# Keys and values of the memory formed before its norm's root, and the steps around them reordered

## The reference

```python
h = rmsnorm(x, g_mix);  mem_n = rmsnorm(mem, g_mem)
proj = h @ w_in                       # HGRN2 | dilated attention | memory queries | three gates
kv = mem_n @ w_mem_kv                 # keys and values of the memory, 4 heads of 128 each
p_m = softmax(q_m @ k_m^T * 128**-0.5);  o_mem = p_m @ v_m
f = lb + (1 - lb) * sigmoid(z)        # lb: softmax over two rows of logits, per direction
x = x + merged @ w_out                # merged: three branches, each with its sigmoid gate
x = x + PEER(rmsnorm(x));  out = rmsnorm(x)
# rmsnorm(x, g) = x * rsqrt(mean(x * x) + 1e-6) * g, the mean over the 2048 features
```

## Time and profile before

| | |
|---|---|
| median of three runs | 4317.9 us |
| profiled execution | 4321.06 us, span 4319.3 us, mean granted TensorE clock 0.992 |
| TensorE (PE) busy | 4240.2 us, 98% |
| its weight loads (PEld) | 3881.8 us, 90% |
| DVE | 2501.7 us, 58% |
| ACT | 1574.3 us, 36% |
| POOL | 2529.4 us, 59% |
| DMA | 870.50 MB, 202 GB/s on average |

### The profile page before, as it was taken

One profiled execution on the slowest core, in us unless ns is written; L12 is line 12 of the kernel. 1 busy time (PEld: TensorE's weight loads), 2 busy tenths in 40 slices (PEclk: granted clock), 3 DMA queues, 4 the chain that ended last, 5 costly groups with the idle time before them and its releaser, 6 DMA issues.

```text
span 4319.3 us, 67486 instructions
## 1 busy us (share of the span) xinstructions
PE 4240.2 (98%) x24940; PEld 3881.8 (90%) x24940; DVE 2501.7 (58%) x3662; ACT 1574.3 (36%) x2079; POOL 2529.4 (59%) x1276
## 2 busy tenths in 40 slices
PE   7999999999999999999999999999989999999998
PEld 7878788888887877888899999999989999999998
DVE  5422443455535433897477777777762467766655
ACT  5222333333334433222344444444433332333332
POOL 5333344444443444444588888887008898898773
PEclk9999999999999999999999999999999999999999
DMA  7695566666667874233355555555365799999983
GB/s 251 203 382 170 152 202 186 192 187 189 190 189 225 269 228 136 88 97 120 118 123 136 132 123 135 131 134 133 122 214 175 274 342 336 333 345 349 346 297 108
DMA packets 574119, 870.50 MB, mean 202 GB/s; under 512 B 85648, under 2 KB 423952, under 8 KB 556944
## 3 DMA queue, kind: packets, MB, share of 16 engines
q1 hardware_dynamic: 401536, 591.47, 42.9%
q0 software_dynamic: 77824, 134.52, 11.7%
q10 hardware_dynamic: 94608, 142.52, 9.3%
HBM read 784.55 MB, written 218.04 MB: 232 GB/s over the span
## 4 chain that ended last, share of the span: by engine, by line
PE 80%; issue 9%; POOL 6%; DVE 2%; DMA 2%; ACT 1%; ACTq 0%; POOLq 0%; DVEq 0%; SPq 0%
PE banks L2076 18%; PE banks L2077 18%; PE banks L2078 18%; PE banks L2413 7%; PE banks L2414 7%; PE banks L2412 7%; POOL w_lo L682 4%; POOL w_lo L738 1%; PE banks L2277 1%; DMA arena<-expert_rows_scratch,constants 1%; POOL constants L720 0%; DVE arena L1391 0%; DMA constants<-gelu_scratch 0%; PE banks L2372 0%; DMA w_raw<-w_u 0%
## 5 line engine op out<-in xcount | busy, mean ns | idle before, releaser
L2076 PE MATMUL banks<-x_hi,w_hi 128*128 128x512 f32 (+1 forms) x4800 | 1777.0, 370 | 29.9 <-DVE x_lo L1997 13.2
L2077 PE MATMUL banks<-x_lo,w_hi 128*128 128x512 f32 (+2 forms) x4928 | 1798.3, 365 | 0.0
L2078 PE MATMUL banks<-x_hi,w_lo 128*128 128x512 f32 (+1 forms) x4800 | 1761.4, 367 | 0.0
L682 POOL TENSOR_TENSOR w_lo<-w_raw,w_hi 128x1024 fp32r<-128x1024 f32 x364 | 898.7, 2471 | 1436.3 <-ACT w_hi L752 1232.3
L752 ACT ACTIVATE w_hi<-w_raw 128x1024 fp32r<-128x1024 f32 x612 | 644.8, 1058 | 1070.2 <-PE banks L2078 1000.1
L2076 PEld LDWEIGHTS banks<-x_hi,w_hi 128*128 128x128 f32 x4800 | 904.8, 188 | 144.6 <-DVE x_lo L1997 14.9
L2077 PEld LDWEIGHTS banks<-x_lo,w_hi 128*128 128x128 f32 x4928 | 931.4, 189 | 104.5 <-issue 1.2
L2078 PEld LDWEIGHTS banks<-x_hi,w_lo 128*128 128x128 f32 x4800 | 904.7, 188 | 109.7
L705 POOL DMA_INDIRECT gate_matrix_scratch<-arena,constants x384 | 741.5, 1931 | 116.9 <-issue 116.9
L738 POOL TENSOR_TENSOR w_lo<-w_raw,w_hi 128x1024 fp32r<-128x1024 f32 x252 | 611.0, 2433 | 133.6 <-ACT w_hi L752 131.3
L2414 PE MATMUL banks<-x_hi,w_lo 128*128 128x256 f32 x1664 | 470.8, 283 | 0.0
(11 more groups left out here) (291 smaller groups left out, 4527.1 us busy)
## 6 DMA issues: line engine op xcount, KB each, us to landing
expert_rows_scratch<-w_v SPq DMA_DIRECT2D x256, 512.0 KB, 5.2
w_raw<-w_u SPq DMA_DIRECT2D x256, 512.0 KB, 3.7
w_raw<-w_v SPq DMA_DIRECT2D x256, 512.0 KB, 5.1
w_raw<-w_in SPq DMA_DIRECT2D x200, 512.0 KB, 3.7
gelu_scratch<-arena ACTq DMA_DIRECT2D x126, 256.0 KB, 2.5
gate_matrix_scratch<-early_mix_or_one_hots SPq DMA_DIRECT2D x16, 1536.0 KB, 9.7
constants<-gelu_scratch ACTq DMA_DIRECT2D x128, 192.0 KB, 6.3
early_mix_or_one_hots<-gate_matrix_scratch ACTq DMA_DIRECT2D x32, 768.0 KB, 10.7
```

The lines of the kernel that those rows point to most:

```text
L682: nc.gpsimd.tensor_tensor(wlo[s][:], raw[s][:], whi[s][:], ALU.subtract).then_inc(w_lo_made, 1)
L2076: M.matmul(out, whi[s][:, k], h, start=f, stop=False)
L2077: M.matmul(out, whi[s][:, k], l, start=False, stop=False)
L2078: ins = M.matmul(out, wlo[s][:, k], h, start=False, stop=e)
```

## The change

The gain of the memory's norm is still multiplied into each tile before it is rounded, in ACT's rounding itself; the root is left out of the tiles. It is one number per memory token, so it is multiplied into the keys and values as they are copied out of PSUM, now by DVE (`key_value_out`), from a copy of the spread root in SBUF (`mem_root`). The squares of the memory are taken two tiles at a time, 512 columns, after the first weights have been rounded; its mean is taken by TensorE behind half 4 of the `w_kv` stream and spread behind half 5 (chunk `c == 2`), the input's mean behind half 8 and spread behind half 9 (`c == 4`). The first key chunks are formed one at a time, in banks 0, 1, 6, 5, 0, 1, 0, 1. The memory's operands move: low parts into the early mix buffers, high parts into the last eight tiles of `xlo`, so the input's first eight low parts need no wait for `w_kv`. All of the memory's low parts are made by DVE. The copies of chunks 4 to 7 stand between DVE's operations on the input. Parameters and first constants are queued between the two halves of the memory. The lower bounds' first six operations move behind the input's norm, their exponential before the memory attention, the last seven behind it.

The core of the diff (left out: imports of names, semaphore lists and the memory attention's neighbours, which do not change):

```diff
+KV_BANK = [0, 1, 6, 5, 0, 1, 0, 1]
+        mlo = nc.alloc_sbuf_tensor_at("memory_low", [P, KT, MEM], F32R, offset=nc.sbuf_base - 4 * HT * T)
-        mhi = xlo[:, :, 0:MEM]
-        mlo = xlo[:, :, MEM:2 * MEM]
+        mhi = xlo[:, HT:KT].rearrange("p k (h t) -> p (k h) t", h=2)
+        mem_root = carve(13312, MEM)
@@ POOL
-            low_halves(0, 4)
-            odd_tiles(0, src_mem, mhi, mlo)
-            low_halves(4, 2 * C_PQ + 4)
+            low_halves(0, 2 * C_PQ + 4)
@@ ACT
+            load_memory(0)
+            act.dma_start(prm[:], params).then_inc(consts_in, 16)
             act.dma_start(cst[:, 0:C_DM], const[:, 0:C_DM]).then_inc(consts_in, 16)
-            act.dma_start(prm[:], params).then_inc(consts_in, 16)
+            load_memory(1)
...
+            def memory_hi(tiles):
+                for k in tiles:
+                    if k % HT == 0:
+                        act.wait_ge(mem_in[k // HT], 16)
+                    norm[0][0].done(A.activation(mhi[:, k], src_mem[:, k], ACT.Copy,
+                                                 scale=prm[:, P_MEM + k:P_MEM + k + 1]), f"hi{k}")
+            def memory_squares(pairs):
+                for k in pairs:
+                    square_tile(0, src_mem.rearrange("p (a b) t -> p a (b t)", b=2), k, T)
+            act.wait_ge(norm_constants, 2)
+            A.activation(small[:, 77:78], epsilon, ACT.Sqrt)
+            round_half(0, 0, first=True)
+            act.wait_ge(consts_in, 32)
+            memory_hi(range(0, 6))
+            round_half(0, 1, first=True)
+            memory_hi(range(6, 12))
+            round_half(0, 2, first=True)
+            memory_hi(range(12, KT))
+            round_half(0, 3, first=True)
+            beside = [
+                (lambda: memory_squares(range(0, 4)), lambda: memory_squares(range(4, 8))),
+                (lambda: None, lambda: (norm_root(0, MEM), input_squares(range(0, 3)))),
+                (lambda: input_squares(range(3, 6)), lambda: input_squares(range(6, 9))),
+                (lambda: input_squares(range(9, 12)), lambda: input_squares(range(12, 15))),
+                (lambda: input_squares(range(15, 16)), lambda: norm_root(1, T)),
+                (lambda: input_hi(range(0, 3)), lambda: input_hi(range(3, 6))),
+                (lambda: input_hi(range(6, 9)), lambda: input_hi(range(9, 12))),
+                (lambda: input_hi(range(12, 15)), lambda: input_hi(range(15, 16)))]
             for c in range(N_KV):
+                for part in range(2):
+                    ahead(c, 0, 2, part)
+                    beside[c][part]()
@@ DVE
+            for k in range(KT):
+                norm[0][0].wait(dve, f"hi{k}")
+                norm[0][1].done(V.scalar_tensor_tensor(mlo[:, k], src_mem[:, k], prm[:, P_MEM + k:P_MEM + k + 1], mhi[:, k],
+                                                       ALU.mult, ALU.subtract), f"lo{k}")
+            for k in range(HT - 1):
+                sum_tile(0, k, T)
+            norm[0][0].wait(dve, "sqrt")
+            norm[0][1].done(V.reciprocal(rms[0][:, 0:MT], rms[0][:, 0:MT]), "rcp")
+            dve.wait_ge(means, 2)
+            V.tensor_copy(mem_root, norm_bank(0)[:, 0:MEM]).then_inc(norm_constants, 1)
+            def key_value_out(c):
+                dve.wait_ge(half_done, 2 * c + 2)
+                V.tensor_tensor(kvm[:, c], mem_root, bank[KV_BANK[c]][:, 0:MEM], ALU.mult).then_inc(acc_free, 1)
+            for c, tiles in ((0, ()), (1, range(0, 5)), (2, range(5, 10)), (3, range(10, 15))):
+                key_value_out(c)
+                for k in tiles:
+                    sum_tile(1, k, T)
+            norm_rest(1, src_x, T, P_MIX, xhi, xlo, {k: key_value_out for k in (4, 5, 6, 7)})
@@ norm_rest: key_value_out(4), (5) and (6) before input tiles 0, 6 and 15; then low parts 0 to 7,
   key_value_out(7), low parts 8 to 15
@@ TensorE
             for c in range(N_KV):
+                if c >= 4:
+                    pe.wait_ge(acc_free, c - 1 if c < 6 else c + 1)
                 if c == 3:
+                    pe.wait_ge(summed[0], HT - 1)
+                for x in range(2):
+                    half(2 * c + x, (2 * c + x) % 4, bank[KV_BANK[c]][:, 0:MEM], list(range(8)), 8 * x, x == 0, x == 1,
+                         width=MEM, his=mhi, los=mlo, ready=tiles_split(0) if c == 0 else None).then_inc(half_done, 1)
+                    if c == 2:
+                        if x == 0:
+                            mean_of_squares(0, MEM, HT - 1)
+                        else:
+                            spread(0, MEM)
+                    if c == 4:
+                        if x == 0:
+                            pe.wait_ge(acc_free, 5)
+                            mean_of_squares(1, T, KT - 1)
+                        else:
+                            spread(1, T)
```

More of the change, by code:

```diff
@@ L399, in square_slot @@
         def square_slot(r, k, width):
-            if k < KT - 1 and r < 2:
-                return bank[2 + k % 4][:, 0:width]
+            if r == 0 and k < HT - 1:
+                return bank[2 + k % 4]
+            if r == 1 and k < KT - 1:
+                return bank[2 + k % 3]
             return nsq[:, k % 2, 0:width]
         def square_slots(r):
-            return 4 if r < 2 else 2
+            return (4, 3, 2, 2)[r]
         def norm_bank(r):
@@ new lines, in memory_squares, with input_squares, input_hi @@
+            def memory_squares(pairs):
+                for k in pairs:
+                    square_tile(0, src_mem.rearrange("p (a b) t -> p a (b t)", b=2), k, T)
+            def input_squares(tiles):
+                for k in tiles:
+                    if k % HT == 0:
+                        act.wait_ge(x_in[k // HT], 16)
+                    square_tile(1, src_x, k, T)
+            def input_hi(tiles):
+                for k in tiles:
+                    norm_hi(1, src_x[:, k], k, xhi[:, k])
@@ L851, in gate_store @@
                 act.dma_start(gate_dram[tile], gst[:, b]).then_inc(gate_out[b], 16)
+            act.wait_ge(lb_dve, 6)
+            A.activation(lbs[:, 24:48], lbs[:, 0:24], ACT.Exp).then_inc(lb_act, 1)
             for h in range(MH):
@@ L1390, in norm_rest @@
                 for k in range(KT):
+                    if r == 1 and k in (0, 6, 15):
+                        beside[4 + k // 6](4 + k // 6)
                     nd_.done(V.scalar_tensor_tensor(src[:, k], src[:, k], prm[:, gcol + k:gcol + k + 1],
@@ L1407, in _ @@
[L1407 to L1415 removed]
+                    beside[7](7)
+                    for k in range(HT, KT):
+                        lo(k)
@@ new lines, in _ @@
+            norm[0][1].done(V.reciprocal(rms[0][:, 0:MT], rms[0][:, 0:MT]), "rcp")
+            dve.wait_ge(means, 2)
+            V.tensor_copy(mem_root, norm_bank(0)[:, 0:MEM]).then_inc(norm_constants, 1)
+            dve.wait_ge(norm_constants, 3)
+            def key_value_out(c):
[3 more added lines that the diff above has]
+                key_value_out(c)
+                for k in tiles:
+                    sum_tile(1, k, T)
@@ L1460, in _ @@
             save_output(MH - 1)
+            dve.wait_ge(lb_act, 1)
+            for d in range(2):
+                link(V.tensor_tensor(sm[:, d], ex[:, d, 0], ex[:, d, 1], ALU.add))
+            link(V.reciprocal(sm, sm))
+            for d in range(2):
+                link(V.tensor_tensor(lbt[:, :, 2 * d], ex[:, d, 0], sm[:, d], ALU.mult))
+            for d in range(2):
+                link(V.tensor_scalar(lbt[:, :, 2 * d + 1], lbt[:, :, 2 * d], -1.0, 1.0, ALU.mult, ALU.add))
             dve.wait_ge(masks_in, 32)
@@ L2099, in mean_of_squares @@
             def mean_of_squares(r, width, sums):
-                last = square_slot(r, KT - 1, width)
+                count = HT if r == 0 else KT
+                last = square_slot(r, count - 1, T)
                 pe.wait_ge(summed[r], sums)
-                pe.wait_ge(squared[r], KT)
+                pe.wait_ge(squared[r], count)
                 for tt in range(width // P):
-                    for s, part in enumerate((nrm, last)):
-                        ins = M.matmul(norm_bank(r)[:, tt:tt + 1], part[:, P * tt:P * tt + P], one_over_d,
-                                       start=(s == 0), stop=(s == 1))
+                    parts = [(v, at) for v in (nrm, last) for at in range(P * tt, T, width)]
+                    for s, (part, at) in enumerate(parts):
+                        ins = M.matmul(norm_bank(r)[:, tt:tt + 1], part[:, at:at + P], one_over_d,
+                                       start=(s == 0), stop=(s == len(parts) - 1))
                 ins.then_inc(means, 1)
```

87 lines of the change are left out of this document (15 added, 72 removed).

## The result

The changed kernel takes 4327.08 us (median of 12 runs, 4324.63 to 4330.21), the kernel before on the same chip 4317.18 us (12 runs, 4313.56 to 4325.45). The ratio is 1.0020, with an interval of 1.0013 to 1.0028: slower by 9.9 us, within 0.3%. The prediction had called for 4317, with a range that ended at 4325; the measured time lies 2 us above it.

A forecast was written before the change was run, and what follows sets the result against it. TensorE, busy 98% of the span, was the bound; only its waits at the start could give time. The pair's first half ending at 89.5 against 90.2 gave -0.7: 4317.9 - 0.7 = 4317.2 us, range 4308 to 4325.

The forecast's parts named there:

- end of half 1: TensorE's second half of key and value products, at the start, was to end at 20.5 us.
- half 5's weights landed: Weights of key and value half 5 were to land at 27.9 us, the same time as before the change.
- memory's mean, start: TensorE, after half 4, was to stand from 29.2 until DVE's sum at 31.5 us, then take the memory's mean.
- DVE's input sums, start and end: DVE's 15 sums of input squares, behind the spread and copies, were to run from 41.2 to 53.7 us.
- hole before the input's mean: TensorE, behind half 8, was to wait 6 us for the last square, where 1.04 us was before.
- eight input low parts, start and duration: After scaling tile 15 at 76.5 us, DVE was to make eight input low parts by 82.9, 0.80 us each.
- last value copy done: DVE's copy of the last value chunk, behind eight input low parts, was to free the pair's second accumulator at 83.3 us.
- first half of the pair: First half of the first memory-query pair: 5.44 us from 83.3, later if at 1.2 GHz; middle taken, ending at 89.5.
- the duration of DVE's low parts: Low parts were to take 0.47 us per memory tile, lagging rounding under 0.5 us, and 0.80 us per input tile.
- Rival 2: Slower, 20%: halves 1 to 4 at 1.2 GHz or half 5's weights over 3 us later; +2 to +5 us.
- Rival 1: The lead is kept, 25%: holes at the means close, the pair starts some 7 us earlier; -4 to -10 us.
- The clock: TensorE's slow starts: 1.6 us charged after both means, half before the pair; none gives -4 us, one more +3.

The follow-up runs named there:

- dve_first_lows: Changed kernel with the first four low halves of weights made by DVE between its low parts, not by POOL: 4321.44 us, ratio 1.0010 to the kernel before.
- pair_lows_dve: Changed kernel with low halves 16 to 19 of the weights made by DVE instead of POOL: 4322.08 us, ratio 1.0016 to the kernel before.
- kv7_early: Changed kernel with the last value copy behind the input's second low part instead of its eighth: 4320.39 us, ratio 1.0009 to the kernel before.
- combo_order: combo with the input's squares and sums begun earlier and ACT's two roots one step earlier: 4311.10 us, ratio 0.9977 to the kernel before.
- best: combo_order with low halves 16 to 19 on DVE, mostly behind low parts 7 and 11, and the last value copy behind low part 3: 4308.63 us, 0.9979.
- combo: Changed kernel with the edits of dve_first_lows and kv7_early together: 4316.24 us, ratio 0.9991 to the kernel before.
- The probe: Layer's computation left out; DVE operations timed alone, then beside POOL's low halves: two-SBUF-operand subtraction 0.72 to 2.23 us, fused operation 0.51 to 2.47 us.
- filler: Changed kernel with 24 unused products of 512 columns in TensorE's hole before the pair: 4325.76 us, ratio 1.0016 to the kernel before.

## Why the prediction was wrong

By its own steps, predicted against measured:

| step | predicted | measured |
|---|---|---|
| first wide product | 12 | 11.83 |
| end of half 1 | 20.5 | 28.7 |
| half 5's weights landed | 27.9 | by 28.8 |
| memory's mean, start | 31.5 | 37.6 |
| DVE's input sums, start and end | 41.2, 53.7 | 44.0, 56.5 |
| hole before the input's mean | 6 | 5.1 |
| that mean | 1.95 | 3.54 |
| end of half 9 | 60.6 | 64.8 |
| eight input low parts, start and duration | 76.5, 6.4 | 80.5, 11.2 |
| last value copy done | 83.3 | 92.0 |
| first half of the pair | 6.2 | 8.5 |
| its end | 89.5 | 100.6 |

(When half 5 landed in the changed kernel is not shown, as its rounding there waited for half 1. Its load went out at 16.62 us, where the prediction kept the 14.5 of the kernel before though it put low half 1, which frees the slot, at 16.8.)

The start was right: the first tile rounded at 10.54 where 10.8 was said, the first product at 11.83. The hole before the input's mean, its reason (the sums stand behind the spread, the root copy and two key copies), the wait for the spread (1.57 us) and the place where the pair is held (the last value copy) were right too.

**The step that failed is the duration of DVE's low parts**, twice. "DVE follows each tile with a low part (0.47), which fits beside 0.40 to 0.42 but for a lag under 0.5 us" became 12.24 us for ten. The 0.47 was the price of another operation, the scaling in L1391, one of whose operands lies in PSUM. In the kernel before, eight of the memory's low parts were POOL's own, and of DVE's eight only the first met a low half of weights (1.17 us where the others took 0.42). The change gave all to DVE and left POOL with weights alone. TensorE then waited for low parts four times (5.6 us), mostly in half 1, the granted clock fell to 0.50, and half 1 ended 8 us late. TensorE in stretches of 4 us, changed kernel:

```profile
16.00:20.00 4.00, 1.48 (x10) 0.91 1.01 425
20.00:24.00 4.00, 2.02 (x6) 0.50 0.95 401
24.00:28.00 4.00, 2.86 (x13) 0.50 1.03 434
```

From there the delay went through TensorE's own order. Half 5 was rounded late too (28.80), but DVE's sums of the memory were ready at 32.65; halves 2, 3 and 4 ended only at 37.6, and the memory's mean followed them without a wait:

```profile
37.59 1.84 PE L2142 MATMUL banks<-small,arena 128*128 128x1 f32 x16
```

That is 6.1 us late. Half 5 then ran at full clock (2.8 us where 4.7 were forecast), so that the spread, the sums of the input and its mean came some 3 to 4 us late. (The forecast start of the sums, 41.2, does not follow from its terms: 39.0 and three operations of 0.42 make 40.3.) dve_first_lows shows the whole: 5.9 us of the 10.4 come back with it.

The second time is "it makes eight low parts by 82.9", from 12.80/16 = 0.80 us. In the kernel before, POOL had two operations in that stretch (77.67 and 80.40 us), and TensorE waited for the first two low parts only (1.78 and 1.75 us). After the change three of POOL's lie beside the first eight (one at 80.19, two in 5.67 us from 83.07): 11.21 us. As the last value copy stands behind them in DVE's order, TensorE waited 7.4 us instead of 2.8, and started at 1.2 GHz. pair_lows_dve shows it (4.90 us, third copy 5.1 us earlier). kv7_early shows that it is the copy's place, and not only its slowness, that costs: 6.0 us come back by moving that one copy. These two overlap: on top of an early copy, freeing the pair's stretch gave only 2.1 us more (combo_order's 94.69 to best's 92.63). combo, with the first four low halves and the copy's place alone, takes back 12.2 us, more than the 10.4 that were lost.

Against its own schedule the kernel is 2.8 us late at the start of the input's sums, 4.2 at the end of half 9, 4.0 at the input's low parts, 8.7 at the last value copy and 11.1 at the end of the pair's first half. So the two stretches of low parts make 2.8 and 4.7 us of the 11.1 directly; the rest is mostly the clock.

Rival 2 foretold this chain ("the mean, the spread, DVE's first sum and the second mean all come later by the same amount"), but with the clock or half 5's weights as its start, and priced at 2 to 5 us. The clock did fall there, behind the waits for low parts; the only wait for a transfer of weights in the changed kernel is 1.4 us, for half 4. Rival 1, that the lead is kept, is what the same change gives once DVE's low parts are freed and the copy and the sums moved ahead: best has it, at 92.63 - 10.87 = 81.8 us.

The clock was under-priced as well: I charged 1.6 us behind the input's mean and 0.8 before the pair. The mean itself was slow, 3.54 for 1.95 us, as the clock had fallen in the 5.1 us hole before it (granted 0.68 from 52 to 56 us, 0.50 from 56 to 60); and the pair's first half took 2.3 us more than predicted. These rows show the mean, the start of half 9 and the spread:

```profile
56.59 3.54 PE L2142 MATMUL banks<-small,arena 128*128 128x1 f32 x16 [5.11 <-DVE arena L1363]
59.99 0.56 PE L2110 MATMUL banks<-x_lo,w_hi 128*128 128x256 f32 x1
...
66.29 1.16 PE L2149 MATMUL banks<-constants,small 128*128 128x128 f32 x8 [1.57 <-DVE small L1391]
```

The clue had been in the rows I quoted: the two tensor-scalars of 4.72 us that ended with POOL's 4.77. I took that for a stall of those two only, and used an average for the input's low parts, and another operation's price for the memory's, without asking for their spread. The Trainium skill names the mechanism (SBUF — State Buffer, "Who interferes with whom"): the two engines share a pair of ports as an exclusive lock, and "a DVE instruction with two SBUF inputs contends with a GpSimd instruction that reads SBUF", while one with at most one SBUF input does not outside certain modes. The probe agrees: 2.23 and 2.47 us with two such inputs, no change with one in PSUM. Its tensor-scalars have one SBUF input and were stretched too (0.20 to 0.92 us); whether they run in one of those modes no run shows.

## What to carry over

Before moving elementwise work to DVE, look at where its operands lie and at what POOL does in that stretch: an operation with two SBUF operands costs up to one whole POOL operation (here 2.4 us for 0.5), so its price is min, median and max of its form, never an average taken where POOL rested. Give both kinds of work in such a stretch to DVE alone (a low half took 1.22 us there, 2.4 on POOL), or read one operand from PSUM. Last, put the copy that frees TensorE's accumulator ahead of work that TensorE needs only later.

## What the runs showed of the hardware

- The stall does not depend on the size of DVE's operation: 128x256 and 128x512 both came out at one POOL operation apiece (2.47 and 2.23 us), and POOL, too, was touched only now and then (its 24 operations took 2.34 us but for single ones up to 2.85).
- A hole's length alone does not tell the clock behind it: 2.05 us (filler) kept 1.00, 2.2 us (pair_lows_dve) was followed by a mean of 0.63 over 4 us, and 5.1 and 7.4 us by 0.50. What TensorE did before differs among them, and no run here separates the two. In the kernel before, two holes of 1.78 and 1.75 us, 2.7 us apart, were followed by products 0.43 us apart from 84.3 us on, and in combo_order, where both copies and low parts lie otherwise, a hole of 1.8 us was not. The Trainium skill (TensorE: Matmul & The Clock Gate, "What's actually happening") names two states, full and half, and the trace agrees: the 7.4 us hole was followed by 0.50, and the 0.63 is a mean over a change, as the products of pair_lows_dve stand 0.23 us apart until 88.8 us and 0.43 from 89.0.
- A mean made of products with one column gains about as much from the clock as wide ones: 1.84 us at a granted 1.00, 3.54 us at 0.50; products of 256 columns stood 0.12 and 0.21 us apart.
